# The head of a two-layer block: normalise x token-major and transpose it on TensorE, with all shift dots on VectorE

## What is computed

```python
c_act = jax.nn.silu(c)
for l in range(2):
    mod = (c_act @ ada_w[l] + ada_b[l]).reshape(bsz, 6, 1024)[:, :, None, :]
    shift_m, scale_m, gate_m = mod[:, 0], mod[:, 1], mod[:, 2]
    shift_f, scale_f, gate_f = mod[:, 3], mod[:, 4], mod[:, 5]
    # rms_norm(x, g) = x * rsqrt(mean(x*x, axis=-1) + 1e-6) * g
    h = rms_norm(x, mix_pre_g[l]) * (1.0 + scale_m) + shift_m
    proj = h @ w_in[l]            # q, k, v, x_lru, gate
    y = ...                       # rope, attention, recurrence, group norms, @ w_out
    x = x + gate_m * rms_norm(y, mix_post_g[l])
    h = rms_norm(x, ffn_pre_g[l]) * (1.0 + scale_f) + shift_f
    x = x + gate_f * rms_norm(conv_ffn(h, ...), ffn_post_g[l])
```

## Time and profile before

| what | value |
|---|---|
| median of 3 runs | 1144.2 us (1143.95 to 1145.02) |
| profiled execution, its own time | 1144.63 us |
| its span, first to last instruction | 1142.8 us |
| mean granted TensorE clock | 0.991 |
| PE busy | 1116.1 us, 98% of the span |
| DVE busy | 803.2 us, 70% |
| ACT busy | 567.4 us, 50% |
| GpSimd busy | 51.9 us, 5% |
| bytes moved by DMA | 159.88 MB, 140 GB/s on average |

### The profile page before, as it was taken

The page is one execution under the profiler, slowest core; times in us unless marked ns, Lnnn a source line. Parts: engine busy times, 40 slices in busy tenths (PEclk is TensorE's granted clock), DMA queues, the critical chain, the costliest instruction groups (busy, mean ns, idle before and its releaser), DMA issues.

```text
span 1142.8 us, 14253 instructions
## 1 busy us (share of the span) xinstructions
PE 1116.1 (98%) x5638; PEld 936.3 (82%) x5638; DVE 803.2 (70%) x1229; ACT 567.4 (50%) x958; POOL 51.9 (5%) x110
## 2 busy tenths in 40 slices
PE   6999999999999999999999999999999999999997
PEld 6986777988888888888889778898888888888886
DVE  7999987776678876588576897777643655356545
ACT  4488948644124422244387895774422434134431
POOL 3100110000111011000000000000000000000000
PEclk7999999999999999999999999999999999999999
DMA  9853273334675547643232422323322332233231
GB/s 355 333 216 111 93 275 130 116 106 148 235 266 195 179 157 272 203 153 128 74 111 79 89 74 74 107 79 102 102 92 92 101 102 75 93 120 102 92 92 74
DMA packets 49284, 159.88 MB, mean 140 GB/s; under 512 B 9409, under 2 KB 9665, under 8 KB 49217
## 3 DMA queue, kind: packets, MB, share of 16 engines
q1 hardware_dynamic: 33968, 118.57, 30.6%
q0 software_dynamic: 10368, 37.75, 9.9%
q10 hardware_dynamic: 4880, 2.64, 0.9%
HBM read 156.83 MB, written 2.11 MB: 139 GB/s over the span
## 4 chain that ended last, share of the span: by engine, by line
PE 82%; DVE 7%; ACT 5%; DMA 3%; issue 2%; SPq 0%; DVEq 0%; ACTq 0%
PE ps L1834 48%; PE ps L1859 33%; DMA sb_raw<-in_w 2%; DVE sb_wL L1147 1%; DMA sb_vw<-in_ada 1%; ACT sb_wH L604 1%; DVE sb_x L1225 1%; PE ps L1947 1%; ACT sb_sq L736 1%; DVE sb_y L1192 1%; PE ps L2124 0%; ACT sb_I L835 0%; DVE sb_y L1199 0%; DVE sb_y L1239 0%; DVE sb_xc L1454 0%
## 5 line engine op out<-in xcount | busy, mean ns | idle before, releaser
L1834 PE MATMUL ps<-sb_hH,sb_wH 128*128 128x512 f32 x832 | 325.7, 391 | 0.3 <-DVE sb_R L1776 0.3
L1834 PE MATMUL ps<-sb_hL,sb_wH 128*128 128x512 f32 x832 | 323.9, 389 | 0.0
L1834 PE MATMUL ps<-sb_hH,sb_wL 128*128 128x512 f32 x832 | 323.9, 389 | 0.0
L1147 DVE TENSOR_TENSOR sb_wL<-sb_raw,sb_wH 128x1024 fp32r<-128x1024 f32 x182 | 221.2, 1220 | 87.1 <-ACT sb_wH L604 86.9
L604 ACT ACTIVATE sb_wH<-sb_raw 128x1024 fp32r<-128x1024 f32 x182 | 189.6, 1053 | 161.2 <-DMA sb_raw<-in_w 161.0
L1859 PE MATMUL ps<-sb_wH,sb_mH 128*128 128x512 f32 x512 | 202.5, 396 | 3.6 <-DVE sb_wL L1147 2.7
L1859 PE MATMUL ps<-sb_wL,sb_mH 128*128 128x512 f32 x512 | 199.7, 390 | 0.0
L1859 PE MATMUL ps<-sb_wH,sb_mL 128*128 128x512 f32 x512 | 199.6, 390 | 0.0
L1834 PEld LDWEIGHTS ps<-sb_hH,sb_wH 128*128 128x128 f32 x832 | 156.2, 188 | 37.6 <-issue 3.6
L1834 PEld LDWEIGHTS ps<-sb_hH,sb_wL 128*128 128x128 f32 x832 | 156.2, 188 | 32.8
L1834 PEld LDWEIGHTS ps<-sb_hL,sb_wH 128*128 128x128 f32 x832 | 156.2, 188 | 31.7
(11 more groups left out here) (222 smaller groups left out, 1135.0 us busy)
## 6 DMA issues: line engine op xcount, KB each, us to landing
sb_raw<-in_w SPq DMA_DIRECT2D x182, 512.0 KB, 3.5
sb_adaw<-in_ada POOLq DMA_DIRECT2D x42, 512.0 KB, 4.7
sb_stage<-in_ada SPq DMA_DIRECT2D x24, 512.0 KB, 14.3
sb_vw<-in_ada POOLq DMA_DIRECT2D x20, 512.0 KB, 5.2
sb_raw<-in_w SPq DMA_DIRECT2D x8, 384.0 KB, 14.3
sb_stage<-in_ada POOLq DMA_DIRECT2D x6, 512.0 KB, 3.8
sb_x<-in_x SPq DMA_DIRECT2D x4, 512.0 KB, 5.9
sb_x<-in_xt SPq DMA_DIRECT2D x4, 512.0 KB, 6.6
```

Of the source, the lines that this page charges most:

```text
L1147: TT(low_of(n), raw_of(n), high_of(n).bitcast(fp32), ALU.subtract).then_inc(w_lo, 1)
L1834: return nc.tensor.matmul(out, a, b, start=start, stop=stop, **kw)
```

## The change

- `x` is loaded once, token-major, in the first load; the second load and the wait for it (L513 to L515, L1221) are gone.
- ACT squares each token tile with the sum carried along (`first_square`), takes the root (`first_root`), DVE takes the reciprocal and scales tiles 0 to 2 (`first_scaled`); ACT scales tile 3. `norm_cols`, the additions, and the first `norm_spread` are gone.
- PE transposes block kt of the scaled x, 4 transposes of 128 x 128, into bank 6 (`first_transposes`); for block kt + 1 this stands in the middle of block kt's high products, and waits until ACT has read block kt out of bank 6 (`tmp_ready`).
- ACT writes `hH` and `rt` = bank 6 * gain + shift itself, two reads of bank 6; DVE's L1300 is gone and its L1312 becomes a plain subtraction that waits for both.
- `PE_SHIFT` is empty: DVE makes all 16 dots in the loop.
- The first half of the softplus chain (`softplus_exp`) moves on ACT from before the loop to after block 2, its DVE part from block 0 to after block 2's angles; the rope tables stand behind both writes of block 3.
- `gw` is loaded after the last transposes; the waits for freed stage slots count DVE's dots only.
- Half 0 of blocks 6 and 7 is done block by block: 18 matmuls of block 6, then a wait for block 7, then 18.

```diff
-PE_SHIFT = (1, 3, 5, 7)
+PE_SHIFT = ()
@@ SyncE
-            part = KT * SEQ // 4
-            for h in range(4):
-                sp.dma_start(x[:, h * part:(h + 1) * part], A["x"][:, h * part:(h + 1) * part]).then_inc(x_in[h], 16)
+            for t in range(QT):
+                sp.dma_start(x_tile(t), A["xt"][tile_of(t), :]).then_inc(x_in[t], 16)
...
-            sp.wait_ge(presq_used, 3)
-            sp.dma_start(gw[:, :, :], A["gw"][0]).then_inc(gw_in, 16)
...
-            sp.wait_ge(tmp_ready, KT)
-            for t in range(QT):
-                sp.dma_start(x_tile(t), A["xt"][tile_of(t), :]).then_inc(xt_in, 16)
+            sp.wait_ge(first_turned, KT)
+            sp.dma_start(gw[:, :, :], A["gw"][0]).then_inc(gw_in, 16)
@@ ScalarE
+            act.wait_ge(consts, 3)
+            fetch_sqrt()
+            def first_square(t):
+                act.wait_ge(x_in[t], 16)
+                nc.scalar.activation(first[t], x_tile(t), ACT.Square, accum_out=xsum[:, t:t + 1]).then_inc(first_sum, 1)
+            def first_root(t, total):
+                act.wait_ge(first_sum, total)
+                nc.scalar.activation(sd8[:, t:t + 1], xsum[:, t:t + 1], ACT.Sqrt, bias=eps,
+                                     scale=1.0 / D).then_inc(first_sd, 1)
+            first_square(0)
+            first_root(0, 1)
+            first_square(1)
+            first_root(1, 2)
             act.wait_ge(csil_mm, 1)
             nc.scalar.activation(csb[:, :], bank(6, 2), ACT.Copy).then_inc(csb_ready, 1)
...
+            first_square(2)
+            first_root(2, 3)
+            first_square(3)
+            first_root(3, 4)
+            act.wait_ge(first_rs, 4)
+            nc.scalar.activation(first[3], x_tile(3), ACT.Copy, scale=rs8[:, 3:4]).then_inc(first_hat[3], 1)
...
             for kt in range(KT):
                 act.wait_ge(slab_in[kt], 16)
                 nc.scalar.activation(slab_of(wH, kt), slab_of(raw, kt), ACT.Copy).then_inc(slab_hi, 1)
+                act.wait_ge(first_turned, kt + 1)
+                act.wait_ge(shift_ready, kt + 1)
+                if kt >= 4:
+                    act.wait_ge(lo_ready, kt - 3)
+                shift, gain = mod[:, 0, kt:kt + 1], fac[:, 0, 0, kt:kt + 1]
+                nc.scalar.activation(hH[:, kt, :], bank(6), ACT.Identity, bias=shift, scale=gain).then_inc(hi_ready, 1)
+                nc.scalar.activation(rt(kt), bank(6), ACT.Identity, bias=shift, scale=gain).then_inc(tmp_ready, 1)
+                if kt == 2:
+                    softplus_exp()
                 if kt == 3:
                     rope_tables()
-                act.wait_ge(shift_ready, kt + 1)
-                act.wait_ge(tmp_ready, kt + 1)
-                nc.scalar.activation(hH[:, kt, :], rt(kt), ACT.Identity, bias=mod[:, 0, kt:kt + 1],
-                                     scale=1.0).then_inc(hi_ready, 1)
@@ VectorE
+            def first_scaled(t):
+                dve.wait_ge(first_sd, t + 1)
+                nc.vector.reciprocal(rs8[:, t:t + 1], sd8[:, t:t + 1]).then_inc(first_rs, 1)
+                if t < QT - 1:
+                    dve.wait_ge(first_rs, t + 1)
+                    TS(first[t], x_tile(t), rs8[:, t:t + 1], None, ALU.mult).then_inc(first_hat[t], 1)
...
+            def slab_low(kt):
+                dve.wait_ge(slab_hi, kt + 1)
+                TT(slab_of(wL, kt), slab_of(raw, kt), slab_of(wH, kt).bitcast(fp32), ALU.subtract).then_inc(slab_lo, 1)
...
-                STT(out=rt(kt), in0=xt(kt), scalar=fcol, in1=bank(6), op0=ALU.mult, op1=ALU.mult).then_inc(tmp_ready, 1)
...
+                    dve.wait_ge(stage_in[2 * kt + 1], 16)
+                    dot_unit(stage[:, 2 * kt + 1, :], 0, kt)
                     dve.wait_ge(ada_used, used)
                     sums = mod[:, 0, kt:kt + 1]
+                self_wait()
                 TT(mod[:, 0, kt:kt + 1], sums, bias_col(0, kt, 1), ALU.add).then_inc(shift_ready, 1)
...
+                if kt not in PE_SHIFT:
+                    slab_low(kt)
                 dve.wait_ge(hi_ready, kt + 1)
-                STT(out=hL[:, kt, :], in0=rt(kt), scalar=mod[:, 0, kt:kt + 1], in1=hi_of(hL)[:, kt, :],
-                    op0=ALU.add, op1=ALU.subtract).then_inc(lo_ready, 1)
+                dve.wait_ge(tmp_ready, kt + 1)
+                TT(hL[:, kt, :], rt(kt), hi_of(hL)[:, kt, :], ALU.subtract).then_inc(lo_ready, 1)
@@ TensorE
+            def first_transposes(kt):
+                if kt:
+                    pe.wait_ge(tmp_ready, kt)
+                for t in range(QT):
+                    if kt == 0:
+                        pe.wait_ge(first_hat[t], 1)
+                    last = nc.tensor.transpose(bank(6)[:, t * P:(t + 1) * P], first[t][:, kt * P:(kt + 1) * P], ident[:, :])
+                last.then_inc(first_turned, 1)
...
                     for c in range(GRP):
                         a, al = block_pair(c, kt)
+                        if c == GRP // 2:
+                            first_transposes(kt + 1)
...
+                first_transposes(KT - 1)
                 for h in range(2):
...
+                    for kts in ([KT - 2], [KT - 1]) if h == 0 else ([KT - 2, KT - 1],):
+                        for c in range(GRP):
+                            for kt in kts:
```

More of the change, by code:

```diff
@@ L184, in build @@
         sqb = [sq[:, :], work[:, SEQ:2 * SEQ]]
-        presq = [scr[:, :], vwf, work[:, :], gw[:, :, :].rearrange("p a b -> p (a b)")]
+        first = [scr[:, :], vwf, work[:, :], gw[:, :, :].rearrange("p a b -> p (a b)")]
         EARLY = range(2 * KT, 3 * KT)
@@ L493, in early_fill, with rows_used @@
                 sp.dma_start(early_slots[i], A["ada"][EARLY[i]]).then_inc(unit_in[i], 16)
-            sp.wait_ge(ada_used, 2)
+            def rows_used(kt):
+                sp.wait_ge(ada_used, 2 * (kt + 1) - sum(1 for s in PE_SHIFT if s <= kt))
+                if kt in PE_SHIFT:
+                    sp.wait_ge(shift_mm, PE_SHIFT.index(kt) + 1)
+            rows_used(0)
             early_fill(0)
             early_fill(1)
-            sp.wait_ge(ada_used, 5)
+            rows_used(2)
             early_fill(4)
@@ L683, in _, with softplus_exp @@
             nc.scalar.activation(ctmp, craw, ACT.Exp, scale=-1.0).then_inc(c_exp, 1)
[L684 to L687, removed]
+            act.wait_ge(consts, 3)
[11 more added lines that the diff above has]
+            first_root(1, 2)
             act.wait_ge(csil_mm, 1)
             nc.scalar.activation(csb[:, :], bank(6, 2), ACT.Copy).then_inc(csb_ready, 1)
[L690 to L696, removed]
+            first_square(2)
[4 more added lines that the diff above has]
+            nc.scalar.activation(first[3], x_tile(3), ACT.Copy, scale=rs8[:, 3:4]).then_inc(first_hat[3], 1)
+            def softplus_exp():
+                act.wait_ge(params_in, 16)
+                lam = par[:, :, COLS["lam"]:COLS["lam"] + LT]
+                S.mark(nc.scalar.activation(sp1[:, :, :], lam, ACT.Abs))
+                self_wait()
+                nc.scalar.activation(sp2[:, :, :], sp1[:, :, :], ACT.Exp, scale=-1.0).then_inc(sp_exp, 1)
             def rope_tables():
@@ L1317, in _ @@
                     TS(ang, ang, PI, -PI, ALU.min, ALU.max).then_inc(ang_ready, 1)
+                    dve.wait_ge(sp_exp, 1)
+                    link(TS(sp1[:, :, :], sp2[:, :, :], 2.0, None, ALU.add))
+                    nc.vector.reciprocal(sp1[:, :, :], sp1[:, :, :]).then_inc(sp_recip, 1)
             lo_chunk(GRP)
@@ L1899, in first_group @@
                             pair_mm(pair_acc(IN_, h, c), al, hH[:, kt, part_of(h)], False, False)
+                    if kt == 0 and 1 in PE_SHIFT:
+                        shift_sums(1)
                     if kt + 2 in PE_SHIFT:
@@ L2032, in pair_passes, with norm_spread @@
                             token_products(l, stage, fh, t, kt, kt == 0, ready if t == 0 else None)
-            def norm_cols():
-                pe.wait_ge(ssq_ready, 1)
-                for t in range(QT):
-                    last = mm(bank(7)[:, t:t + 1], ssq[:, t * P:(t + 1) * P], ones[:, 0:1], True, True)
-                last.then_inc(cols_ready, 1)
-            def norm_spread(m, b, rs=rs8):
-                if m:
-                    pe.wait_ge(g_copied, m * LT)
-                pe.wait_ge(rs_ready, m + 1)
+            def norm_spread(m, b, rs):
+                pe.wait_ge(g_copied, m * LT)
+                pe.wait_ge(rs_ready, m)
                 for t in range(QT):
```

76 lines of the change are left out of this document (26 added, 50 removed).

## The result

The changed kernel takes 1147.21 us (median of 7 runs, 1146.60 to 1149.25) against 1144.2 (7 runs, 1143.57 to 1145.97) on the same chip: ratio 1.0026, interval 1.0014 to 1.0037. It is 3 us slower. The forecast was 1147.3. The profiled execution took 1147.91 of its own, with a span of 1146.1 (1144.63 and 1142.8 before), so the two traces differ by 3.3.

A forecast was written before the change was run, and what follows sets the result against it. PE was taken to bound the head before, DVE's stream with its waits for ACT after. PE delay 2.0 plus clock 1.5 less 0.4 absorbed gave +3.1, so 1147.3 us as median; range 1143.8 to 1149.2.

The forecast's parts named there:

- What bounds the kernel: Head: PE bound it before the change, with DVE close behind; afterwards PE catches up by block 3 and waits for DVE.
- Start of the loop: Before block 0: ACT's last root at 13.5 us, DVE's first dot at 13.9, range 13.7 to 14.6.
- One block on DVE: DVE's loop: period 5.1 us, bounds 4.4 and 5.3, with a new 0.7 us wait for ACT's second write.
- rival with the smaller wait: Each block's subtraction: DVE's wait for ACT is smaller, period below 4.84 us, 1142.1 at 4.6; chance 0.14.
- Added once: DVE's loop, once only: angles 3.44 us, softplus steps 0.4, and a 1.0 us stall at block 4 from ACT's rope tables.
- End of the head: After block 7: DVE ends at 59.5 us, 54 matmuls take 6.5, so PE finishes at 66.1, 2.0 late.
- the low clock lasts: Start of the head: PE stays at half clock past block 0, up to 2.6 us more, 1149.5; chance 0.11.
- Clock: PE's 2.9 us idle before block 7: clock falls, some 3 us of matmuls at half speed, 1.5 us more.
- clock stays up: Gap before block 7: no clock fall, PE and DVE both 2.0 us late, nothing absorbed, 1146.3; chance 0.27.
- Absorbed: Near 90 us: a later PE absorbs its waits for DVE and ACT, about 0.4 us in all, 0.33 of it shown.
- Sum: Whole kernel: 2.0 + 1.5 less about 0.4 gives +3.1 us, 1147.7 profiled, 1147.3 as median; chance 0.48.
- second load of x: Near 65 to 70 us: removing this 2 MB transfer gains nothing, since no wait of PE hangs on it.

The follow-up runs named there:

- e2: Changed kernel with DVE's scale dot of the next block moved ahead of the current block's subtraction: 1141.42 us, ratio 0.9977 to the kernel before.
- e5: Changed kernel with DVE's next scale dot ahead of the subtraction and ACT's rope tables ahead of block 3's writes: 1139.42 us, ratio 0.9968 to the kernel before.
- e6: Changed kernel with the shift dots of blocks 3, 5 and 7 back on PE: 1144.05 us, ratio 1.0005 to the kernel before.
- e4: Changed kernel with ACT's rope tables put ahead of block 3's two writes: 1147.05 us, ratio 1.0019 to the kernel before.
- e1: The changed kernel run again without edits, yardstick for three other runs on its chip: 1147.03 us, ratio 1.0021 to the kernel before.
- e3: Changed kernel with eleven unused 512-column matmuls put into PE's wait before block 7: 1146.42 us, ratio 1.0017 to the kernel before.
- e7: Changed kernel with half 0 of blocks 6 and 7 done in one sequence again: 1149.70 us, ratio 1.0056 to the kernel before.
- e8: Changed kernel with the second load of x and DVE's wait for it put back behind the gw load: 1147.15 us, ratio 1.0036 to the kernel before.

## Why the prediction was right

**What bounds the kernel.** That PE bounded the head before, with DVE close behind, rests on the earlier trace rows (PE busy in 28.30 of 28.30 us) and was not tried by a run. That DVE bounds it after is shown by e2, e5 and e6: less DVE time per block moves the tile forward, and 5.1 us more PE time (e6) does not hold it back.

**Start of the loop.** 13.9 was forecast, the dot starts at 13.29. The term was the cost of a tile on ACT: its square and root hold ACT 1.38 us (squares start at 10.16 and 11.54), not 1.49, since the small root gives the engine free after 0.20 of its 0.29. So the last root ends at 12.99 and not 13.5. How near the number came is partly chance: in the nine traces with this code the loop starts between 13.20 and 14.03, by the arrival of `x`, and the forecast of 13.9 lies within that.

**One block on DVE.** 5.1 forecast, 5.12 measured; the new wait for ACT 0.7 forecast, 0.72 to 0.78 measured. This step carries the verdict. It came from two rows: the shape of ACT's scaled PSUM read (0.78) and DVE's slab (0.96). The rival with the smaller wait needed a period under 4.84 and had no row for it.

**Added once.** Angles and softplus 3.84 forecast, 3.77 measured (the dots of blocks 2 and 3 are 8.89 apart). The rope tables cost 1.0; 0.97 measured (6.09 from dot to dot instead of 5.12), and e4 removes just that.

**End of the head.** DVE 59.5 forecast, 58.96 measured, the 0.6 of the start. The first product 17.6, measured 17.19. Four transposes 0.55, measured 0.44 (0.11 from start to start). PE had caught up by block 3: it waits 2.19 us for it. The tile was put at 66.1 at full clock; by the measured signal it is 65.66. The delay of 2.0 was therefore 1.56, a mis-size that comes from the start of the loop. In e1, where the loop starts 0.36 later, the same sum gives 1.89. The clock at the start rose near 22.6 us (starts 0.12 apart from there on), 23.0 was expected, so the rival *the low clock lasts* did not come about.

**Clock.** 1.5 us forecast, 1.57 measured, with the fall where it was expected and e3 showing that the gap is its cause. The row that it was argued from, though, was weaker than the text made it: the same transposes after the same wait of 1.23 us, at 0.57 of the clock in the earlier trace rows, run undisturbed in the trace of the changed kernel:

```profile
138.97 1.06 PE L2155 MATMUL ps<-sb_ident,sb_adaw 128*128 128x128 f32 x8 [1.23 <-DVE sb_mL L1526]
```

That wait of 1.23 us stands before these transposes in all ten traces, and the clock fell in the wait or within 1.3 us behind it in five (before, e2, e6, e7, e8) and in the other five not. By that row alone the rival "clock stays up" at 0.27 was a fair one. Before block 7 the fall came in all five traces with a wait of 2.7 us or more and in none of the three with 0.84 to 1.46. What the Trainium skill says of waits between bursts ("TensorE: Matmul & The Clock Gate", "HAM oscillation — how this bites in real kernels") held for these long gaps; for the wait of 1.23 us the runs show both outcomes.

**Absorbed.** 0.4 forecast, 0.13 measured: PE's wait for DVE at the transposes fell from 0.33 to 0.20 and not to nothing, because DVE's ropes were late too, by 1.43 (67.22 against 65.79). The text had both numbers, ropes 2.0 late beside a PE 3.5 late, and DVE's date should have capped the absorption.

**Sum.** 2.0 + 1.5 - 0.4 = 3.1 forecast; 1.56 + 1.57 - 0.13 = 3.00 measured at the transposes, 3.3 at the end. So part of the agreement is luck: the delay was 0.4 too large and the absorption 0.3 too large. That the second load of x gives nothing held for the head (e8). That `gw` and GpSimd's later chain cost nothing is seen only from there being no wait of PE for them; no run tried it.

## What to carry to other kernels

When work moves from a busy engine to two others, write down one period of each engine's stream with its waits before counting what is saved; a step that an engine must wait for inside its own loop (here some 0.75 us in seven of eight blocks) is paid in full, and an instruction of the next round put into the wait takes it back (e2). An idle gap of 2 to 3 us on TensorE ahead of a dense stretch is to be priced twice, once as time and once as clock, if the engine has no wait behind it that takes up the loss. A gain at the front of a kernel can shrink before its end, where a transfer with its own date stands between (e3 and e4 gave back about half, e2 and e5 nothing).

## What the runs showed of the hardware

- The clock after a wait of TensorE, in profiled executions. Before block 7: waits of 2.72 to 2.74 (the changed kernel, e1, e4, e8) and of 4.53 us (e7) came with a fall to 0.50; waits of 0.84, 1.41 and 1.46 (e5, e6, e2) with none. Before block 3: waits of 2.19, 2.27, 2.18, 3.08 and 3.15 us (the changed kernel, e7, e8, e3, e4) were followed by some 3 us at 0.50, one of 2.42 (e1) was not, nor were 0.58, 0.91 and 1.60 (e6, e2, e5). The same wait of 1.23 us near 131 to 141 us was followed by a fall in five traces of ten. What else decides was not found.
- The fall comes at no fixed place: inside the wait (block 7 of e7, at 0.50 from 57 us on, the wait ends at 59.06), with the first matmul behind it (block 3 of the changed kernel, 0.55 us instead of 0.36), or 1.1 to 1.3 us behind that matmul (block 7 of the changed kernel, block 3 of e3 and e4).
- The fall at block 3 cost nothing in the changed kernel: in e1, without it, PE then waited 1.31 us for block 4's slab; with it, the wait was used up.
- A matmul of 256 columns takes 0.12 us from start to start at 1.00 and 0.21 at 0.50.
- ACT's read of PSUM with scale and bias is 0.78 us for 512 columns, and the next starts 0.68 after it.
